# Old states' products and the last tile's mLSTM norm moved into the output projection, and the normaliser column joined to the prompt's state products

## The reference

```python
num = a[..., None] * jnp.einsum('bhvk,blhk->bhlv', C0, q) + jnp.einsum('bhls,bshv->bhlv', wqk, v)
den = a * jnp.einsum('bhk,blhk->bhl', n0, q) + wqk.sum(-1)
h = num / jnp.maximum(jnp.abs(den), jnp.exp(-m))[..., None]
...
CL = aL[..., None, None] * C0 + jnp.einsum('bhs,bshv,bshk->bhvk', ws, v, k)
nL = aL[..., None] * n0 + jnp.einsum('bhs,bshk->bhk', ws, k)
```

## Time and profile before

| | |
|---|---|
| Median of 3 runs | 2012.08 us |
| The runs | 2007.52, 2012.08, 2012.95 us |
| The profiled execution | 2008.96 us |
| Its span, first to last instruction | 2007.3 us |
| TensorE busy | 1906.9 us, 95% |
| VectorE busy | 1419.5 us, 71% |
| ScalarE busy | 685.2 us, 34% |
| Mean granted clock of TensorE | 0.957 |

### The profile page before, as it was taken

One profiled execution on the slowest core, in us unless ns is written; L12 is line 12 of the kernel. 1 busy time (PEld: TensorE's weight loads), 2 busy tenths in 40 slices (PEclk: granted clock), 3 DMA queues, 4 the chain that ended last, 5 costly groups with the idle time before them and its releaser, 6 DMA issues. The chain is left out here.

```text
span 2007.3 us, 28106 instructions
## 1 busy us (share of the span) xinstructions
PE 1906.9 (95%) x9473; PEld 1537.7 (77%) x9473; DVE 1419.5 (71%) x3020; ACT 685.2 (34%) x1170; POOL 276.3 (14%) x229
## 2 busy tenths in 40 slices
PE   6999999899999968888999999999999999999996
PEld 3455456765666637887999889999999999999996
DVE  4112256453268899997888897877878787878786
ACT  1222254211111114674333443433333333333332
POOL 0000000010011000001111112122323232323210
PEclk9998989698899978999999999999999999999998
DMA  7300010273234152558786778788989898989872
GB/s 272 133 0 1 0 38 1 73 230 136 89 102 131 49 186 85 241 205 342 288 319 234 296 258 326 256 325 321 355 321 356 318 358 318 358 318 358 318 273 77
DMA packets 135162, 434.81 MB, mean 217 GB/s; under 512 B 12385, under 2 KB 70162, under 8 KB 111186
## 3 DMA queue, kind: packets, MB, share of 16 engines
q1 hardware_dynamic: 108978, 256.69, 35.3%
q0 software_dynamic: 26112, 177.22, 23.1%
HBM read 399.21 MB, written 34.27 MB: 216 GB/s over the span
## 5 line engine op out<-in xcount | busy, mean ns | idle before, releaser
L1522 POOL DMA_INDIRECT hi<-euv,lo x160 | 241.6, 1510 | 1009.8 <-DVE hi L2107 754.6
L1098 PE MATMUL ps<-xh,ul 128*128 128x384 f32 x1024 | 347.7, 340 | 0.0
L1098 PE MATMUL ps<-xl,uh 128*128 128x384 f32 x1024 | 346.5, 338 | 0.0
L1098 PE MATMUL ps<-xh,uh 128*128 128x384 f32 x1024 | 344.3, 336 | 0.0
L1162 ACT ACTIVATE hi<-ps 128x512 f32<-128x512 f32 (+12 forms) x312 | 174.0, 628 | 262.4 <-PE ps L761 82.8
L1106 PE MATMUL ps<-vh,hh 128*128 128x512 f32 x768 | 239.9, 394 | 4.3 <-DVE hl L2048 4.3
L1106 PE MATMUL ps<-vh,hl 128*128 128x512 f32 x768 | 238.2, 391 | 0.0
L1106 PE MATMUL ps<-vl,hh 128*128 128x512 f32 x768 | 236.7, 389 | 0.0
L1162 ACT ACTIVATE vh<-lo 128x1024 fp32r<-128x1024 f32 x128 | 135.8, 1061 | 260.9 <-PE ps L1106 251.2
L2107 DVE SCALAR_TENSOR_TENSOR hi<-hi,lo 128x1024 f32<-128x1024 f32 x160 | 198.5, 1282 | 7.6
L1098 PEld LDWEIGHTS ps<-xl,uh 128*128 128x128 f32 x1024 | 192.7, 188 | 5.5
(11 more groups left out here) (327 smaller groups left out, 2420.7 us busy)
## 6 DMA issues: line engine op xcount, KB each, us to landing
lo<-eu SPq DMA_DIRECT2D x128, 512.0 KB
lo<-ev SPq DMA_DIRECT2D x128, 512.0 KB
gates<-hi SPq DMA_DIRECT2D x6, 4096.0 KB, 12.2
hi<-gates SPq DMA_DIRECT2D x62, 384.0 KB, 6.1
hi<-w_pq SPq DMA_DIRECT2D x8, 2048.0 KB, 8.2
hi<-w_in SPq DMA_DIRECT2D x5, 2048.0 KB, 12.6
hi<-cache SPq DMA_DIRECT2D x64, 144.0 KB, 2.5
hi<-cache POOLq DMA_DIRECT2D x64, 144.0 KB, 2.7
```

Of the source, the lines that this page charges most:

```text
L1098: last = nc.tensor.matmul(ps[:, 6 + p, 0:ND * TD], a[p][:, k * 128:(k + 1) * 128], b[:, k, :], start=(k == 0 and b is xh and a is uh), sto ...
L1522: nc.gpsimd.indirect_dma_start(ring[slot].rearrange("p a d -> p (a d)"), None, euv, bass.IndirectOffsetOnAxis(at, 0)).then_inc(r_in[slot], 16)
```

## The change

- The old states' products (`old_states`: lines 838 and 841 before) stand behind group 0 of the projection, and their turns (`old_turned`) behind group 1. The queries that they need are copied by ScalarE to `mqS` before `wo` overwrites them, and SP's load of `wo` waits for that copy (`sws_exp` 2) instead of the products (`inter_ps`).
- The pairs of `new_states` stand behind the groups 1 to 4, where they stood behind 0 to 3.
- VectorE's part moves with them: `old_parts` behind the first residual; `last_norm` (`numi`, `ml_den`, `ml_norm` of tile 4) behind the second residual and the first two new states; tile 4's gate behind the first layer norm. The copy of bank 7 to `hbuf` stays ahead.
- ScalarE's square root for tile 4 stands behind its eight copies to `xm`.
- `vw` has 129 columns a head, the last one the weight itself, so line 866 goes: three heads' results lie in bank 0, the fourth's in bank 1, and four copies bring them to `cst`.
- The sequences' normaliser product writes bank 4 instead of 6.

```diff
--- before.py
+++ after.py
@@ -204,12 +204,14 @@
         assert H0 + KD * 512 + NT + 4 * TR <= H0 + TI * D and XT0 + 8 * MH * TR + 4 * TR <= H0
-        vw = view(CT + MH * SB * DH, 2, MH * DH, rows=TR)
+        vw = view(CT + MH * SB * DH, 2, MH, DH + 1, rows=TR)
...
         cst = view(Q0 + 2 * NT, MH * DH + MH)
...
         WPQ = 38244
+        mqS = view(Q0 + 704, MH, NS)
         zkS, zvS = view(QRT, 512, rows=NS), view(QRT + 512, 512, rows=NS)
@@ -463,7 +465,7 @@
             sp.wait_ge(s["keep_done"], 1)
-            sp.wait_ge(s["inter_ps"], 1)
+            sp.wait_ge(s["sws_exp"], 2)
             sp.wait_ge(s["ml_qk"], TI * MH)
@@ -831,25 +833,11 @@
             ml_scores(last4 + 1)
-            pe.wait_ge(s["ct_in"], 32)
-            pe.wait_ge(s["sws_lin"], 1)
...
-            last.then_inc(s["inter_ps"], 1)
             ml_turn(last4)
...
             ml_scores(last4 + 3)
-            pe.wait_ge(s["numt_done"], 1)
...
-            last.then_inc(s["numi_ps"], 1)
             ml_values(last4 + 1)
@@ -861,10 +849,9 @@
                     k = zk[:, i, h * 128:(h + 1) * 128]
-                    nc.tensor.matmul(ps[:, 0, h * 128:(h + 1) * 128], k, vw[:, i % 2, h * 128:(h + 1) * 128],
-                                     start=(i == 0 and h == 0), stop=(i == TI - 1), skip_group_check=True)
-                    last = nc.tensor.matmul(ps[:, 1, h:h + 1], k, wsp[:, i, h:h + 1],
-                                            start=(i == 0 and h == 0), stop=(i == TI - 1), skip_group_check=True)
+                    at = h % 3 * (DH + 1)
+                    last = nc.tensor.matmul(ps[:, h // 3, at:at + DH + 1], k, vw[:, i % 2, h, :],
+                                            start=(i == 0 and h % 3 == 0), stop=(i == TI - 1), skip_group_check=True)
                 last.then_inc(s["cst_ps"], 1)
@@ -881,11 +868,28 @@
             pe.wait_ge(s["sws_exp"], 2)
-            pe.wait_ge(s["inter_done"], 1)
             for h in range(MH):
-                last = nc.tensor.matmul(ps[:, 6, h * SB:(h + 1) * SB], zkS[:, h * 128:(h + 1) * 128], wsb[:, h, :],
+                last = nc.tensor.matmul(ps[:, 4, h * SB:(h + 1) * SB], zkS[:, h * 128:(h + 1) * 128], wsb[:, h, :],
                                         start=True, stop=True)
             last.then_inc(s["sst_ps"], 1)
+            def old_states():
+                pe.wait_ge(s["ct_in"], 32)
+                pe.wait_ge(s["sws_lin"], 1)
+                for h in range(MH):
+                    for b in range(SB):
+                        nc.tensor.matmul(ps[:, 6, h * NS + 4 * b:h * NS + 4 * b + 4], ct[:, h * SB + b, :],
+                                         mqS[:, h, 4 * b:4 * b + 4], start=True, stop=True)
+                for h in range(MH):
+                    last = nc.tensor.matmul(ps[0:NS, 6, 256 + h * SB:256 + (h + 1) * SB], mqS[:, h, :], nst[:, h, :],
+                                            start=True, stop=True)
+                last.then_inc(s["inter_ps"], 1)
+            def old_turned():
+                pe.wait_ge(s["numt_done"], 1)
+                for h in range(MH):
+                    last = nc.tensor.transpose(ps[0:NS, 6, h * 128:(h + 1) * 128], numT[:, h, :], ident)
+                last.then_inc(s["numi_ps"], 1)
@@ -893,7 +897,7 @@
                     last = nc.tensor.matmul(ps[:, 2 + b % 2, h * 128:(h + 1) * 128], zkS[:, h * 128:(h + 1) * 128],
-                                            vw[0:NS, b % 2, h * 128:(h + 1) * 128], start=True, stop=True)
+                                            vw[0:NS, b % 2, h, 0:DH], start=True, stop=True)
                 last.then_inc(s["sst_ps"], 1)
@@ -911,9 +915,13 @@
                 last.then_inc(s["wo_ps"], 1)
-                if g < SB // 2:
-                    new_states(2 * g)
-                    new_states(2 * g + 1)
+                if g == 0:
+                    old_states()
+                elif g <= SB // 2:
+                    if g == 1:
+                        old_turned()
+                    new_states(2 * g - 2)
+                    new_states(2 * g - 1)
                 if g % 2 and g > 1:
@@ -1308,11 +1316,11 @@
             act.wait_ge(s["mla_s"], NJ)
+            copy(mqS, mqT[:, :, S0:S0 + NS])
             copy(zkS, zk[0:NS, ST, :])
...
                 ml_pt(n)
-            ml_root(ST)
             for g in range(8):
@@ -1320,6 +1328,8 @@
                 ins.then_inc(s["xm_done"], 1)
+            ml_root(ST)
             def query_copy(b):
@@ -1695,7 +1705,6 @@
                 if i == ST:
-                    step(v.tensor_copy(hbuf, num))
                     step(v.tensor_tensor(hbuf[0:NS], hbuf[0:NS], numi, ALU.add))
@@ -1723,7 +1732,8 @@
                     dve.wait_ge(s["cst_ps"], i - 1)
-                v.tensor_tensor(vw[:, i % 2].rearrange("p (h v) -> p h v", h=MH),
+                v.tensor_copy(vw[:, i % 2, :, DH], wsp[:, i, :])
+                v.tensor_tensor(vw[:, i % 2, :, 0:DH],
                                 zv[:, i, :].rearrange("p (h v) -> p h v", h=MH), bc(wsp[:, i, :], 2, DH), ALU.mult)\
@@ -1758,11 +1768,6 @@
             v.tensor_copy(zs, z0[0:NS, ST, QR:QR + KVR]).then_inc(s["keep_done"], 1)
-            dve.wait_ge(s["inter_ps"], 1)
...
-            step(v.tensor_reduce(nqs, nq, AX, ALU.add))
             ml_weigh(ST * MH + 2)
@@ -1771,34 +1776,47 @@
             weighted_values(1)
-            dve.wait_ge(s["numi_ps"], 1)
-            v.tensor_copy(numi, ps[0:NS, 6, :].rearrange("p (h v) -> p h v", h=MH)).then_inc(s["inter_done"], 1)
-            dve.wait_ge(s["inter_done"], 1)
             dve.wait_ge(s["ml_w"], TI * (MH + 1))
             v.tensor_tensor(sR, bc(am[0:NS, ST, :], 2, SB), bc(const("lastb", rows=NS), 1, MH), ALU.mult).then_inc(s["sel_ready"], 1)
-            ml_den(ST)
             weighted_values(2)
...
             weighted_values(4)
-            ml_norm(ST)
+            dve.wait_ge(s["ml_num"], TI * MH)
+            v.tensor_copy(hbuf, ps[0:TR, 7, :].rearrange("p (h v) -> p h v", h=MH))
             dve.wait_ge(s["cst_ps"], TI)
-            dve.wait_ge(s["ml_num"], TI * MH)
-            v.tensor_copy(cst[:, 0:512], ps[:, 0, :])
-            v.tensor_copy(cst[:, 512:516], ps[:, 1, 0:MH]).then_inc(s["cst_done"], 1)
+            three = ps[:, 0, 0:3 * (DH + 1)].rearrange("p (h v) -> p h v", h=3)
+            v.tensor_copy(cst[:, 0:3 * DH].rearrange("p (h v) -> p h v", h=3), three[:, :, 0:DH])
+            v.tensor_copy(cst[:, 512:515], three[:, :, DH])
+            v.tensor_copy(cst[:, 3 * DH:512], ps[:, 1, 0:DH])
+            v.tensor_copy(cst[:, 515:516], ps[:, 1, DH:DH + 1]).then_inc(s["cst_done"], 1)
             dve.wait_ge(s["sws_exp"], 1)
...
             step(v.tensor_copy(aLb, ps[:, 5, 16:48]))
-            nf = nst.rearrange("p h b -> p (h b)")
-            dve.wait_ge(s["sst_ps"], 1)
-            step(v.tensor_tensor(nf, nf, aLb, ALU.mult))
-            v.tensor_tensor(nf, nf, ps[:, 6, 0:32], ALU.add).then_inc(s["sst_done"], 1)
+            def old_parts():
+                dve.wait_ge(s["inter_ps"], 1)
+                step(v.tensor_tensor(nq, ps[0:NS, 6, 256:288].rearrange("p (h b) -> p h b", h=MH),
+                                     bc(const("selb", rows=NS), 1, MH), ALU.mult))
+                v.tensor_copy(numT, ps[:, 6, 0:128].rearrange("p (h t) -> p h t", h=MH)).then_inc(s["numt_done"], 1)
+                step(v.tensor_reduce(nqs, nq, AX, ALU.add))
+                nf = nst.rearrange("p h b -> p (h b)")
+                dve.wait_ge(s["sst_ps"], 1)
+                step(v.tensor_tensor(nf, nf, aLb, ALU.mult))
+                v.tensor_tensor(nf, nf, ps[:, 4, 0:32], ALU.add).then_inc(s["sst_done"], 1)
+            def last_norm():
+                dve.wait_ge(s["numi_ps"], 1)
+                v.tensor_copy(numi, ps[0:NS, 6, :].rearrange("p (h v) -> p h v", h=MH)).then_inc(s["inter_done"], 1)
+                dve.wait_ge(s["inter_done"], 1)
+                ml_den(ST)
+                ml_norm(ST)
...
                     dve.wait_ge(s["sst_ps"], b)
-                v.tensor_tensor(vw[0:NS, b % 2].rearrange("p (h v) -> p h v", h=MH),
+                v.tensor_tensor(vw[0:NS, b % 2, :, 0:DH],
                                 zvS.rearrange("p (h v) -> p h v", h=MH), bc(wsb[:, :, b], 2, DH), ALU.mult)\
@@ -1822,16 +1840,23 @@
                         .then_inc(s["res_done"], 1)
-                    if 2 * i < SB // 2 and n == 0:
-                        new_state(4 * i)
-                        new_state(4 * i + 1)
+                    if i == 0 and n == 0:
+                        old_parts()
+                    if i in (1, 2) and n == 0:
+                        new_state(4 * i - 2)
+                        new_state(4 * i - 1)
+                if i == 0:
+                    new_state(0)
+                    new_state(1)
+                    last_norm()
                 dve.wait_ge(s["res_done"], 2 * i + 2)
                 layer_norm(hid[:, i, :], i, TI + i, *norm)
-                if 2 * i < SB // 2:
```

(8 more changed lines are left out.)

13 lines of the change are left out of this document (1 added, 12 removed).

## The result

The changed kernel takes 2017.61 us (median of 18 executions, 2015.38 to 2021.32), the kernel before beside it 2010.64 (18, 2007.52 to 2018.11): a ratio of 1.003, 95% interval 1.0021 to 1.0039. The prediction, 2010.0 with a range up to 2013.5, said a gain of 2.1 us; the change costs 7.0.

What follows compares the result with a forecast made beforehand. The prediction took TensorE, busy 95% of the span, as the bound. 17.8 us leaving ahead of the projection less 15.7 us coming into it gave 2.1 us gained: 2010.0 us on the median, range 2003.5 to 2013.5.

Steps and rivals of the forecast that it cites:

- (a): Ahead of the projection: the block of the old states' products goes away, 11.4 us less.
- (b): Last tile's heads behind the old block: the clock stays full, so 6.77 us become 4.25, 2.5 us less.
- (c): Ahead of the projection: the four turns of line 851 go away, 0.44 us less.
- Rival B: Clock not held ahead of the projection, so heads and state products double: 11.3 us lost, 2021.3 us; chance 7%.
- (d): Prompt's state products: twenty one-column products go, the stage taking 5.4 us for 8.92, 3.5 us less (2.7 to 4.0).
- The covers: Ahead of and behind the projection: weights land 4.7 us before need, and first page loads keep 10 us of cover.
- (e): Old states' block behind projection group 0: the same clock split as before, costing 11.4 us (10.3 to 13).
- (f): Projection group 1 starts at half clock after the block: 2.2 us lost (1.8 to 2.7).
- (g): In the projection: the old states' turns, `old_turned`, come in at 0.44 us.
- (h): Behind projection group 3: TensorE waits for VectorE's values for new-state products 4 and 5, 1.7 us (0 to 3).
- Rival A: Clock stays at full in the projection, through the old states' block: 8.2 us gained, 2003.9 us; chance 18%.
- Rival C: TensorE follows VectorE's queue: state-product stage at 6.2 us, new-state wait 3.0 to 4, gain eaten, 2012 us; chance 13%.

Runs made afterwards that it cites:

- dense: The changed kernel with the old states' products turned round, each state moving 128 columns against 32 stationary ones; 2009.71 us, 0.9991 of the kernel before.
- dense_d22: The dense kernel with 2.2 us of needless products (1280 columns) ahead of the last projection group; 2010.9 us, 0.9997 of the kernel before.
- move: The changed kernel with the normaliser's own one-column products again, only the move into the projection left; 2018.2 us, 1.0024 of the kernel before.
- a_d34: The changed kernel with 3.4 us of needless products (1984 columns) ahead of the last projection group; 2018.25 us, 1.0037 of the kernel before.
- column: The kernel before with only the merged 129-column products and their copies; 2014.3 us, 1.0013 of the kernel before.
- b_d34: The kernel before with 3.4 us of needless products (1984 columns) ahead of the last projection group; 2019.4 us, ratio 1.0028.

## Why the prediction was wrong

- **(a), (b), (c), ahead of the projection: right.** The clock is 1.00 from 382.4 to 412.0, through the last tile's small products. Rival B is out.
- **(d) right, a little cautious.** The stage of merged products takes 5.0 us (392.93 to 397.95) for my 5.4. All told 18.2 us left (26.6 instead of 44.9), for my 17.8.
- **The covers held.** The weights landed in 12.9 us (their time in the prediction, 397.5, should read 383.3 + 13.8 = 397.1) and the projection's only wait ahead of its first group is the 0.88 us of before. VectorE's first residual came 3.4 us behind group 0, since it waited for a load of 1 MB (`sub_keys`, 14.5 us to landing), under the block; I had not seen that, and it cost nothing. SP's pages started at 449.7, 18 us behind group 1, and nobody waited for them.
- **(e) 10.1 for 11.4** (411.99 to 422.12), a little below my low end of 10.3: the clock held 4.4 us into the block and not 3.1.
- **(f) 2.1 for 2.2.** Group 1 with its pitch, 422.12 to 431.29, is 9.17 us, where one at full clock is 7.05.
- **(g) 0.5 for 0.4.**
- **(h) 3.3 for 1.7, above the high end of 3.** It is where I put it, behind group 3, for products 4 and 5, and it is 1.6 us long (from group 3's start to the turns behind the pair is 453.4 - 442.8 = 10.6 us, 9.0 in before). What I left out is the clock: behind these two pauses it was at half from 453.9 for 3.4 us, and the turns and group 4 took 1.6 longer. Sum of what came in: 16.1, for 15.7.
- **The sum: 2.1 for 2.1** at the projection's end. Its terms missed by up to 1.6 and nearly cancelled: that the sum agrees so closely is luck.
- **The step that failed** is the sentence behind the sum, on the shift of later stages against their stretches at half clock, "which this sum cannot place", and what I made of it: 4% for a lucky later stage and next to nothing in the range. The runs show 9.3 us lost there, more than four times the gain. It was a term of the sum with a size that the trace of before could have bounded. Its loop lost the clock behind the narrow score products in each of seven rounds, and ran at full behind equally narrow value products in six of them; a fall there costs about 2.3 us by before's own rows (turns 1.65 at half for 0.94, queries 4.87 for 3.27), so the loop had some 6 x 2.3 = 14 us of loss left in it, an estimate. Half of that on the forecast is 2017; the range ended at 2013.5, and slower by over 0.3% had a chance of 6% from quite other causes.
- **Rival A was wrong** in the changed kernel, and the block shows why: no gap, and 0.50 from 416.4. The Trainium skill (TensorE: Matmul & The Clock Gate, section "Why this matters for your kernels") warns against idle gaps between bursts; by that rule alone neither this block nor the loop would have lost the clock. The traces disagree for both: over 546 to 573 us TensorE is busy without a gap at a clock of 0.81. `dense` turns it round: the same gapless block with 128 moving columns keeps 1.00.
- **Rival C was wrong**: VectorE's queue cost 1.6 us of waiting, as I gave it, and not 3 to 4, and stage (d) was paced at 5.0 us and not 6.2.

**Shown and open.** Shown: the loss lies in the loop; it follows the moment of entry, with either order; and it needs the loop's narrow products. Open: which moment is good. My rule, the time from the entry to the first fall of the clock, was taken from ten profiles and missed in the next two (dense_d22's loop was 3 us longer than it said, move's 4 to 7 shorter). Nor does that time alone fix the loop: it is 4.4 us in the changed kernel, a_d34 and `column`, whose loops take 247.8, 244.5 and 244.4. Open too are the 3 to 7 us behind the loop in `column`, `move` and `b_d34`: there the time at half clock behind the loop is 67 to 69 us where before has 61, and one place is a wait for ScalarE. The kernels with wide products take 2.5 to 2.9 us more behind the loop than before does, with TensorE idle for 3 to 5 us more there; what ends those waits stays open.

## What to carry to other kernels

Where TensorE is busy without a gap and its granted clock still falls, look for runs of products with few moving columns. If a product with 128 columns takes as long by the trace as one with 4 or 32, move 128 of them (turn the operands round, or pad with zeros): that gave 0.9% of the whole time in the loop here, where moving work about gave nothing. And before pricing an edit of 2 us, look at the loops behind it: if the clock falls there in each round, a shift alone can be worth more than the edit, in either direction; measure with 1 and 2 us of needless work before believing a small gain or loss.

## What the runs showed of the hardware

- A delay has a price that isn't monotone: 1.2 us of products added made the kernel before 10 us slower, 2.2 us added made the changed kernel 7 us faster.
- The clock fell at 100% busy time behind runs of 4-column and of 32-column products, and did not with 128 columns in the same places; 64 records took 7.2 us with 128 columns at full clock and 9.7 with 4.
- Executions of one and the same kernel can fall into two groups 8 us apart (b_d34: 2012.7 to 2014.2 and 2017.1 to 2023.8), so a median of a few of them may stand for either.
